# Moving the weight buffers and the feed-forward region by fractions of 256 bytes in SBUF

## The reference, cut to what matters

```
def conv_ffn(h, w_up, w_dw, b_dw, w_down):
    u = h @ w_up                       # 1024 -> 5632
    u = causal_dwconv(u, w_dw, b_dw)
    gate, val = jnp.split(u, 2, axis=-1)
    return (jax.nn.silu(gate) * val) @ w_down   # 2816 -> 1024
...
    x = x + jnp.concatenate([mix, mem_o], axis=-1) @ w_out[l]
    x = x + conv_ffn(rmsnorm(x, g_ffn[l]), w_up[l], w_dw_f[l], b_dw_f[l], w_down[l])
```

## Time and profile before

| | |
|---|---|
| median of three runs | 1740.29 us (1738.9 to 1746.7) |
| time of the profiled execution | 1741.23 us |
| its span in the trace | 1739.4 us |
| mean granted clock of TensorE, share of full | 0.992 |
| TensorE matmuls busy | 1673.2 us, 96% of the span, 8728 instructions |
| VectorE, ScalarE, GpSimd busy | 49%, 43%, 41% |
| chain that ended last | TensorE 81%, VectorE 8%, issue 5%, ScalarE 4% |

### The profile page before, as it was taken

How to read it: one execution, slowest core, us unless ns; L and a number is a source line. 1 busy time by engine, 2 the same in 40 slices (tenths; PEclk the granted TensorE clock), 3 DMA queues, 4 the chain that set the end, 5 groups by cost and what they waited for, 6 DMA issues and landing times.

```text
span 1739.4 us, 24060 instructions
## 1 busy us (share of the span) xinstructions
PE 1673.2 (96%) x8728; PEld 1286.2 (74%) x8728; DVE 856.5 (49%) x1349; ACT 743.8 (43%) x1177; POOL 715.3 (41%) x409
## 2 busy tenths in 40 slices
PE   5889899999999999999999999999999998999997
PEld 5656578888888886666788888888876667876666
DVE  7587645555531125434466666311446354456354
ACT  5333443444432234444455555433336543426441
POOL 5433243444444444443434444544324434334431
PEclk9999999999999999999999999999999999999999
DMA  6211222333333332111323233333411112311111
GB/s 226 67 49 50 61 90 89 100 97 96 96 97 100 106 97 73 49 50 37 101 81 96 96 96 96 109 109 97 127 49 49 61 49 85 101 51 61 49 61 49
DMA packets 40107, 143.77 MB, mean 83 GB/s; under 512 B 4448, under 2 KB 4448, under 8 KB 40032
## 3 DMA queue, kind: packets, MB, share of 16 engines
q1 hardware_dynamic: 39024, 139.59, 25.4%
q10 hardware_dynamic: 1008, 3.15, 0.5%
HBM read 140.62 MB, written 2.10 MB: 82 GB/s over the span
## 4 chain that ended last, share of the span: by engine, by line
PE 81%; DVE 8%; issue 5%; ACT 4%; POOL 1%; DMA 0%; POOLq 0%; SPq 0%; DVEq 0%; ACTq 0%
PE banks L1642 22%; PE banks L1644 22%; PE banks L1643 22%; PE banks L1820 3%; PE banks L1855 2%; PE banks L1838 2%; DVE chain L1330 1%; PE banks L1908 1%; ACT prob L701 1%; POOL w_lo L561 1%; DVE nmax L1171 1%; PE banks L1688 1%; PE banks L1689 1%; PE banks L1690 1%; DVE xs_lo L1132 1%
## 5 line engine op out<-in xcount | busy, mean ns | idle before, releaser
L561 POOL TENSOR_TENSOR w_lo<-raw,w_hi 128x1024 fp32r<-128x1024 f32 x255 | 619.1, 2436 | 771.9 <-ACT w_hi L640 771.6
L1642 PE MATMUL banks<-xs_hi,w_hi 128*128 128x512 f32 (+2 forms) x1488 | 600.2, 403 | 12.0 <-DVE xs_lo L1380 4.9
L1644 PE MATMUL banks<-xs_hi,w_lo 128*128 128x512 f32 (+2 forms) x1488 | 579.3, 389 | 0.0
L1643 PE MATMUL banks<-xs_lo,w_hi 128*128 128x512 f32 (+2 forms) x1488 | 578.9, 389 | 0.0
L640 ACT ACTIVATE w_hi<-raw 128x1024 fp32r<-128x1024 f32 x255 | 263.9, 1053 | 287.3 <-PE banks L1644 258.7
L1642 PEld LDWEIGHTS banks<-xs_hi,w_hi 128*128 128x128 f32 x1488 | 281.3, 189 | 85.3 <-issue 17.2
L1644 PEld LDWEIGHTS banks<-xs_hi,w_lo 128*128 128x128 f32 x1488 | 281.0, 189 | 58.4
L1643 PEld LDWEIGHTS banks<-xs_lo,w_hi 128*128 128x128 f32 x1488 | 281.7, 189 | 53.1 <-issue 2.9
L571 POOL TENSOR_SCALAR prob<-prob,rinv 128x512 f32<-128x512 f32 (+3 forms) x144 | 88.5, 627 | 193.0 <-DVE rinv L1180 192.7
L701 ACT ACTIVATE prob<-banks,nmax 128x512 f32<-128x512 f32 (+3 forms) x144 | 83.2, 583 | 176.6 <-DVE nmax L1171 176.4
L1644 PE MATMUL banks<-hid_hi,w_lo 128*128 128x512 f32 x352 | 140.6, 399 | 0.0
(11 more groups left out here) (249 smaller groups left out, 1913.5 us busy)
## 6 DMA issues: line engine op xcount, KB each, us to landing
raw<-wstream SPq DMA_DIRECT2D x255, 512.0 KB, 3.5
x<-xT SPq DMA_DIRECT2D x4, 512.0 KB, 10.7
out<-pt SPq DMA_DIRECT2D x8, 256.0 KB, 2.0
memx<-memT SPq DMA_DIRECT2D x2, 512.0 KB, 7.4
ws_sb<-wsT ACTq DMA_DIRECT2D x2, 512.0 KB, 4.6
qk<-post_rows ACTq DMA_DIRECT2D x2, 512.0 KB, 3.6
sb_sb<-sbT ACTq DMA_DIRECT2D x2, 256.0 KB, 5.2
rope_sb<-rope ACTq DMA_DIRECT2D x1, 512.0 KB, 7.2
```

What stands on the lines that cost most here:

```text
L561: nc.gpsimd.tensor_tensor(w_lo[s][:].rearrange("p k c -> p (k c)"), raw[s][:], w_hi[s][:].rearrange("p k c -> p (k c)").bitcast(f32), SUB) ...
L1642: MM(dst, w_hi[slot][:, k, :], hi, start=start, stop=False)
L1643: MM(dst, w_hi[slot][:, k, :], lo, start=False, stop=False)
L1644: return MM(dst, w_lo[slot][:, k, :], hi, start=False, stop=stop)
```

## The change

The four weight buffers of each kind are put 4096 + 64 bytes apart instead of 4096. The low parts start 32 bytes further than the next step would. And `h0` is moved up to the next address that leaves the remainder by 256 that `xs_hi` leaves. Nothing else is edited: no instruction, wait, loop or size of a transfer. The remainders that follow stand in the table above.

```diff
+LINE = 256
...
         x = put("x", [P, KT, T], f32)
+        xs_at = cursor[0]
         xs_hi = put("xs_hi", [P, KT, T], f32r)
...
-        w_hi = [put(f"w_hi{s}", [P, KT, P], f32r) for s in range(SLOTS)]
-        w_lo = [put(f"w_lo{s}", [P, KT, P], f32r) for s in range(SLOTS)]
+        w_at = cursor[0]
+        w_step = KT * P * 4 + LINE // SLOTS
+        w_hi = [put(f"w_hi{s}", [P, KT, P], f32r, w_at + s * w_step) for s in range(SLOTS)]
+        w_at += SLOTS * w_step + LINE // SLOTS // 2
+        w_lo = [put(f"w_lo{s}", [P, KT, P], f32r, w_at + s * w_step) for s in range(SLOTS)]
+        cursor[0] = w_at + SLOTS * w_step
         fs_at = cursor[0]
...
-        h0 = cursor[0]
+        h0 = cursor[0] + (xs_at - cursor[0]) % LINE
```

## The result

The changed kernel takes 1757.98 us (median of 4, 1757.03 to 1759.38) against 1741.33 us for the kernel before on the same chip. The ratio is 1.0091, with a 95% interval of 1.007 to 1.0113: slower, by about 16 us. The forecast was 1750, slower, with a range of 1716 to 1768.

The account below looks back on a forecast made before the run. The prediction took the time between TensorE's matmul starts as the bound. +14.1 us on `xs` and −3.8 on `hid` gave +10.3; with 1 left out for waits, 1741.2 + 9.3 = 1750.5, given as 1750, range 1716 to 1768.

Parts of the forecast that it names:

- What bounds the kernel: Up and down parts: TensorE never waits, so the time from one matmul's start to the next, 226.7 or 233.3 ns, sets the time.
- The hidden region's term: Down part: moving the hidden region alone takes 1056 matmuls from 233.3 to 226.7 ns, −7.0 us.
- The spread's term: Products: spread weight buffers make a matmul 229.7 ns, +14.1 us on 4704 matmuls, −3.8 us on 1056 with `hid`.
- the six distances that no row showed: Weight loads: distances other than 0 and 96 between weights and moving operand, each taken at 230.0 ns a matmul.
- only the distance of 0 is cheap: Rival for all products: every other distance costs 233.3 ns; +26.1 and −1.2 us, 1765 in all; chance 0.15.
- The sum over single loads: Products: each load priced by its own distance; high 229.2, low 230.8, averaged two to one into 229.7 ns a matmul.
- the prediction's own sign: Up part: the forecast is wrong if slot 0's high loads are no cheaper than the others or units not above 5.44 us.
- What was costed at nothing: ScalarE and GpSimd weight writes stay hidden behind TensorE, VectorE shows no price, DMAs don't move; 256-column matmuls 0.6 us either way.
- The forecast's own range: Whole kernel: 1742 to 1759, from the unknown distances at 227.5 to 233.3 ns a matmul.
- Spreading: Rival for every product: spreading keeps the reads apart, price under 226.7 ns, 1718 or 1695 in all; chance 0.27.
- By 64 alone: Rival for weight loads: only the remainder by 64 counts, high loads 226.7, low 233.3 ns; +5.8 us, 1746; chance 0.08.
- two reads meet somewhere: Each matmul: its read and the next weights' load meet now and then, as often as their address difference sets; 13.3 or 20.0 ns.

## Why the prediction was right, and where it was off

**What bounds the kernel.** Right. The change touched nothing but distances between starts, the instruction counts stayed, and the stretches without waits carried most of the loss. Two readings of the rows were off, without harm to the sum. A 9 in the clock's row means 90% or more, not full clock: for 26.5 us of the first and last stages it was at half. And rows 2 don't exclude all neighbours, since GpSimd was busy for 47% of the down part and 44% of the up part; it was the run with the hidden region alone that excluded them.

**The hidden region's term** (−7.0 us alone) was right: 233.3 became 226.7 ns, and the two down parts of the trace lost 3.5 us each.

**The spread's term** had the right sign and was too small. The forecast had 229.7 ns a matmul for `xs` and `hid` alike; the trace shows 232.4 for both. On the 2112 matmuls of the up parts that is 12.0 us instead of 6.3. On `hid` it is −0.9 ns and −1.0 us instead of −3.8. The step that failed is the value for the six distances that no row showed: 230.0, taken from the middle of two known ones and from a stream that hasn't settled. With high and low loads alike five of them cost 232.3 to 233.9, and only one (192) 229.6. A fair guess from the rows would have been that 0 is the exception, which is the rival "only the distance of 0 is cheap" (233.3 for all else, 1765, chance 0.15). The truth lies between that rival and the forecast, at 1758.

**The sum over single loads** also failed in kind. It gave a load at 0 the cheap price whatever stood around it. The runs with only the low parts moved refute that: beside a load at distance 0 a matmul took 232.6 ns. In the changed kernel itself the matmuls beside a high load take 230.4, 231.5, 232.3 and 230.7 ns in slots 0 to 3. So the prediction's own sign, slot 0's high loads cheaper than the others, holds by 0.3 ns at the least, but they are nowhere near 226.7, and slot 0's units are the second dearest (5.60 us).

**Outside the long parts** the two traces can be compared one by one, since they hold the same 8728 matmuls in the same order. The differences between the steps from one start to the next add up to this (after minus before, us):

```
both up parts, 1008 steps each                             +11.6
both down parts                                             -1.0
elsewhere, 2355 steps of 215 to 245 ns at full clock        +8.7
all other steps at full clock (waits among them)            -1.0
steps that touch a stretch at half clock in either trace    -1.5
start of the first matmul                                   -1.1
sum                                                        +15.8
```

The steps elsewhere grew by 3.7 ns each and not by 5.7, since they started from 228.9 and not from 226.7: the forecast counted all 4704 matmuls from 226.7, while only the 2112 of the up parts were settled there. Waits hid about 1 us, as the forecast had it. The last two terms before the sum are the clock and the start; nothing ties them to the change, and they made the traced loss look smaller. In place of +10.3 the terms that the forecast had in its sum came to +19.3.

**What was costed at nothing** set no time, but VectorE's durations moved. GpSimd's split takes 2404 ns in the up part, where it took 2403. VectorE's busy time fell from 153.6 to 134.8 us in the second up part (the stretches above and the earlier trace rows). Between 885 and 1095 us, 28 of its SCALAR_TENSOR_TENSOR instructions ran beside a split of GpSimd before the change, for 2.0 us each on the mean, and 50 that didn't took 0.75. After it 19 did, for 1.6 us, and 58 didn't, for 0.75. So these instructions were dear only beside a split, at either placement, and fewer of them met one. TensorE was busy without a break in both traces, so it didn't wait for them.

**The range.** 1758 lies inside 1716 to 1768, but that range held a gain, no change and a loss, so the hit says little for the mechanism. The forecast's own range, 1742 to 1759, just held it.

**The rivals.** Spreading gave no better price than equal remainders: no tried distance was under 226.7 ns. By 64 alone it isn't decided either: 64 costs 233.2 where 0 costs 227.1. The page "TensorE: Matmul & The Clock Gate" of the Trainium skill (Part 2, step 1) has two independent read ports, so that loading weights takes nothing from the running matmul; by that rule the time would have stayed at 1740. Here moving nothing but addresses changed a matmul of the up part by 5.7 ns (232.4 against 226.7), and the measurement decides. That two reads meet somewhere, as the prediction took it, is still only inferred: the runs show that the placement sets the interval, not by what mechanism.

## What to carry to other kernels

What follows holds for float32 matmuls of 512 columns with loads of 128 by 128; the runs say little of other shapes. Where TensorE never waits, read the time from one start to the next, to the nanosecond, for each operand: two streams of the same shape at 226.7 and 233.3 ns were worth 7 us here, and the cure was one line of placement. Keep stationary and moving operands that are read together at the same remainder by 256, and leave it so for all buffers of a ring; spreading them over the remainders cost 16 us against the kernel before, and 23 against the one with the hidden region alone (1.0091 / 0.9959 of 1741). Such a price can't be added up load by load, so try a placement as a whole and count units, since one trace shows it to the nanosecond. And before two stages of two traces are compared by their length, look at the granted clock in both: up to 3.4 us of a first stage came from it here.

## What the runs showed of the hardware that I had not expected

- Streams of load and matmul settle into exact cycles: 226.67 ns for each matmul at equal remainders, and patterns of 2, 3, 6 or 7 steps elsewhere, most of them reached within ten matmuls after the buffer changes. Means of 233.3 ns came from patterns as different as (235.8, 230.8) and (232.6, 239.4, 228.0).
- 226.67 and 233.33 ns are 544 and 560 cycles of 2.4 GHz for 512 columns, 32 and 48 over.
- At a distance of 16 bytes the same code at the same addresses ran at 226.9 or at 233.3 ns, by what had run before it.
- The price isn't the same with the roles exchanged: weights at 240 cost 226.7 ns when loaded and 236.5 when they move.
- Loading half the weights, and writing half the rows, for two of three matmuls made the stream slower, 229.3 against 226.7 ns.
- A SCALAR_TENSOR_TENSOR of VectorE beside a split of GpSimd took 2.0 us on the mean, one without a split beside it 0.75.
